# A table of head picks kept on chip, the compression's products set between head sums and transposes, and a memory sum that GpSimd prepares

## The reference, cut to what matters

```python
def rms_norm(x, g):
    return x * lax.rsqrt(jnp.mean(x * x, axis=-1, keepdims=True) + RMS_EPS) * g   # over 64 columns of a head
...
raw = (raw + cmp_pe[None, :, None]).reshape(B, 2, n_cmp, CMP_LEN * HEAD_DIM)      # 31 windows of 32 tokens
hid = jax.nn.gelu(jnp.einsum('bcnf,cfh->bcnh', raw, cmp_w1))                      # c: keys, values; 2048 -> 128
kv_c = jnp.einsum('bcnh,chd->bcnd', hid, cmp_w2)
...
y = ((y - m) * lax.rsqrt(var + GN_EPS)).reshape(B, T, D) * ln_g + ln_b            # group norm, heads of 64
...
memn = rmsnorm(mem, mem_norm_g)                                                   # 256 tokens, over 1024 columns
km, vm = split(memn @ w_kv)
```

## Time and profile before

| | before |
|---|---|
| median of three runs | 2717.42 us (2706.16 to 2719.36) |
| the profiled execution | 2718.71 us |
| its span, first to last instruction | 2716.9 us |
| PE / DVE / ACT / POOL busy | 95% / 44% / 34% / 37% |
| mean granted TensorE clock | 0.952 of full speed |
| moved by DMA | 196.96 MB, 72 GB/s |

### The profile page before, as it was taken

One profiled execution on the slowest core, in us unless ns is written; L12 is line 12 of the kernel. 1 busy time (PEld: TensorE's weight loads), 2 busy tenths in 40 slices (PEclk: granted clock), 3 DMA queues, 4 the chain that ended last, 5 costly groups with the idle time before them and its releaser, 6 DMA issues.

```text
span 2716.9 us, 32275 instructions
## 1 busy us (share of the span) xinstructions
PE 2582.6 (95%) x12202; PEld 1993.1 (73%) x12202; DVE 1193.4 (44%) x2017; ACT 936.8 (34%) x1580; POOL 1016.1 (37%) x611
## 2 busy tenths in 40 slices
PE   7999899999989988899899999999999999999997
PEld 6775477888836667788478788888766787888885
DVE  5112745213052665533253356336359733553362
ACT  3543643222245451222343333222422543322222
POOL 4331435444512221111065254534522452544344
PEclk9998699999989997888799999999999999999999
DMA  3222003333311110000232133323312321233231
GB/s 123 62 62 75 1 24 93 95 99 95 125 39 59 50 47 2 1 1 1 88 118 93 55 94 93 110 83 99 95 62 62 109 88 52 93 93 115 80 99 62
DMA packets 54415, 196.96 MB, mean 72 GB/s; under 512 B 6573, under 2 KB 6701, under 8 KB 53581
## 3 DMA queue, kind: packets, MB, share of 16 engines
q1 hardware_dynamic: 53312, 192.46, 22.9%
q10 hardware_dynamic: 974, 2.76, 0.3%
HBM read 193.10 MB, written 2.10 MB: 72 GB/s over the span
## 4 chain that ended last, share of the span: by engine, by line
PE 44%; DVE 5%; ACT 1%; DMA 0%; issue 0%; SPq 0%; POOLq 0%; POOL 0%; DVEq 0%; ACTq 0%
PE ps L386 10%; PE ps L387 10%; PE ps L388 10%; DVE ps L2815 3%; PE ps L374 3%; PE ps L375 3%; PE ps L376 3%; PE ps L2828 1%; PE ps L2658 1%; PE ps L2681 1%; DVE ps L2977 0%; DMA gwb<-in_lora_b 0%; PE ps L2427 0%; PE ps L2463 0%; PE ps L2434 0%
## 5 line engine op out<-in xcount | busy, mean ns | idle before, releaser
L507 POOL TENSOR_TENSOR w_lo<-raw,w_hi 128x1024 fp32r<-128x1024 f32 x342 | 819.7, 2406 | 1027.3 <-ACT w_hi L480 1027.1
L386 PE MATMUL ps<-ahead_hi,w_hi 128*128 128x512 f32 x1216 | 484.5, 398 | 1.1 <-DVE ahead_lo L609 1.1
L387 PE MATMUL ps<-ahead_lo,w_hi 128*128 128x512 f32 x1216 | 475.2, 391 | 0.0
L388 PE MATMUL ps<-ahead_hi,w_lo 128*128 128x512 f32 x1216 | 474.3, 390 | 0.0
L480 ACT ACTIVATE w_hi<-raw 128x1024 fp32r<-128x1024 f32 x342 | 353.0, 1049 | 171.8 <-PE ps L376 91.0
L386 PEld LDWEIGHTS ps<-ahead_hi,w_hi 128*128 128x128 f32 x1216 | 228.4, 188 | 54.5 <-issue 4.2
L387 PEld LDWEIGHTS ps<-ahead_lo,w_hi 128*128 128x128 f32 x1216 | 228.4, 188 | 51.5 <-issue 4.1
L388 PEld LDWEIGHTS ps<-ahead_hi,w_lo 128*128 128x128 f32 x1216 | 228.3, 188 | 51.0
L620 DVE TENSOR_TENSOR x_stream<-x_stream,ps 128x512 f32<-128x512 f32 x80 | 54.9, 687 | 466.7 <-PE ps L388 268.7
L374 PE MATMUL ps<-ffn_a_hi,w_hi 128*128 128x512 f32 x352 | 137.5, 390 | 2.9 <-DVE ffn_a_lo L2982 2.8
L2949 ACT ACTIVATE ffn_s<-ps 128x512 f32<-128x512 f32 x44 | 26.3, 598 | 326.8 <-DVE ps L2977 326.8
(11 more groups left out here) (419 smaller groups left out, 4772.5 us busy)
## 6 DMA issues: line engine op xcount, KB each, us to landing
raw<-in_wall SPq DMA_DIRECT2D x346, 512.0 KB, 3.6
x_stream<-in_x SPq DMA_DIRECT2D x8, 256.0 KB, 7.5
cw<-in_cmp_w SPq DMA_DIRECT2D x1, 2048.0 KB, 8.0
out_y<-x_stream SPq DMA_DIRECT2D x8, 256.0 KB, 2.2
lora_a<-in_lora_a ACTq DMA_DIRECT2D x1, 1152.0 KB
dist<-in_consts SPq DMA_DIRECT2D x1, 1088.0 KB, 10.0
mem<-in_mem SPq DMA_DIRECT2D x1, 1024.0 KB, 4.9
gwb<-in_lora_b SPq DMA_DIRECT2D x1, 1024.0 KB
```

The source lines that it names most:

```text
L386: pe.matmul(out, hi, src.hi[:, t, 0:width], start=first, stop=False)
L387: pe.matmul(out, hi, src.lo[:, t, 0:width], start=False, stop=False)
L388: return pe.matmul(out, lo, src.hi[:, t, 0:width], start=False, stop=last)
L507: e.tensor_tensor(self.w.lo[:, s, :], self.raw[:, s, :], as_float(self.w.hi[:, s, :]), ALU.subtract).then_inc(lo_r.sem, 1)
```

## The change

- The table of head picks is put a second time into the constants that stay on chip from the start (`own`, 38 columns; that load grows from 1025 to 1063 columns). The head sums and `variance` read it there, and PE's waits for the transfers ahead of them go; ahead of the gate's products a wait for `ld(32)` is added.
- In `prepare_mixers` the transfers are ordered anew: positions, `w1` in two halves of 64 partitions each with a semaphore of its own, then the 1320 constants, `w2`, distances.
- There, too, the ten head sums come first on PE. Behind each of the last four stand eight of the compression's first 32 products; the transposes follow, and behind each turn stand eight of the second 32. ACT squares all ten tiles, takes the root, and copies the turned values afterwards.
- In `GroupNorm` POOL adds the eight squared memory tiles in seven steps into the first, ahead of its two weight chunks, and PE makes one product with ones, behind the last variance.

```diff
-CONST_SIZES = [("ident", 128), ("blockones", 128), ("negtri", 128), ("m4", 512), ("cum", 129),
+CONST_SIZES = [("ident", 128), ("blockones", 128), ("negtri", 128), ("m4", 512), ("cum", 129), ("own", 4 * HEAD_TILES - 2),
...
+            sp.dma_start(pos[:, :], a["cmp_pe"]).then_inc(placed.sem, 16)
+            for half in range(2):
+                rows_ = slice(64 * half, 64 * half + 64)
+                sp.dma_start(w1[rows_, :, :], a["cmp_w1"][rows_, :, :]).then_inc(half_ld[half].sem, 16)
             sp.dma_start(far[:, c - N_KEEP:], a["consts"][:, c:N_CONST]).then_inc(picked.sem, 16)
-            sp.dma_start(pos[:, :], a["cmp_pe"]).then_inc(ld.sem, 16)
-            sp.dma_start(w1[:, :, :], a["cmp_w1"]).then_inc(ld.sem, 16)
             sp.dma_start(w2[:, :], a["cmp_w2"]).then_inc(ld.sem, 16)
...
-            for t in range(n):
-                if t < turns:
-                    turn(t)
-                if t == 0:
-                    pe.wait_ge(picked.sem, picked(16))
-
-                pe.wait_ge(sq_r.sem, sq_r(t + 1))
-                c = at("pick") + rows - 2 - 2 * t
-                pe.matmul(k.ps[0:rows, 0, :], far[:, c:c + rows], sq[:, t % 2, :], start=(t == 0), stop=(t == n - 1)
-                          ).then_inc(ss_r.sem, 1)
-
-            pe.wait_ge(raw_r.sem, raw_r(2))
-            for c in range(2):
+            def hidden(c, first, last):
+
+                if first == 0:
+                    pe.wait_ge(raw_r.sem, raw_r(2))
+                    pe.wait_ge(half_ld[c].sem, half_ld[c](16))
                 o = 64 * c
-                for j in range(32):
+                for j in range(first, last):
                     mm = pe.matmul(k.ps[0:N_CMP, 1 + c, 0:128], raw[o:o + 64, j, :], w1[o:o + 64, j, :],
                                    start=(j == 0), stop=(j == 31))
-                mm.then_inc(hs.sem, 1)
+                if last == 32:
+                    mm.then_inc(hs.sem, 1)
+
+            for t in range(n):
+                pe.wait_ge(sq_r.sem, sq_r(t + 1))
+                c = CST["own"] + rows - 2 - 2 * t
+                pe.matmul(k.ps[0:rows, 0, :], k.consts[:, c:c + rows], sq[:, t % 2, :], start=(t == 0), stop=(t == n - 1)
+                          ).then_inc(ss_r.sem, 1)
+                if t >= n - 4:
+                    hidden(0, 8 * (t - n + 4), 8 * (t - n + 4) + 8)
+            for i in range(turns):
+                turn(i)
+                hidden(1, 32 * i // turns, 32 * (i + 1) // turns)
...
                     pe.wait_ge(hc.sem, hc(1))
+                    pe.wait_ge(ld.sem, ld(16))
...
         @block.vector
         def _(v):
-            v.wait_ge(ld.sem, ld(48))
-
+            v.wait_ge(placed.sem, placed(16))
...
         def variance(m):
             pe.wait_ge(sq.sem, sq(m + 1))
-            if m == 0:
-                pe.wait_ge(ld.sem, ld(32))
-            c = HEAD_TILES * 2 - 2 - 2 * m
-            pe.matmul(k.ps[0:rows, 2, :], self.picks[:, c:c + rows], self.sqt[:, m % 2, :], start=(m == 0),
+            c = CST["own"] + HEAD_TILES * 2 - 2 - 2 * m
+            pe.matmul(k.ps[0:rows, 2, :], k.consts[:, c:c + rows], self.sqt[:, m % 2, :], start=(m == 0),
                       stop=(m == KD - 1)).then_inc(va.sem, 1)
...
-            if m == 4:
-                for n in range(KD):
-                    pe.wait_ge(squared.sem, squared(n + 1))
-                    mm = pe.matmul(k.ps[:, 4, 0:MEM], k.ones[:, :], self.sqm[:, n, :], start=(n == 0), stop=(n == KD - 1))
-                mm.then_inc(summed.sem, 1)
+        pe.wait_ge(self.added.sem, self.added(KD - 1))
+        pe.matmul(k.ps[:, 4, 0:MEM], k.ones[:, :], self.sqm[:, 0, :], start=True, stop=True).then_inc(summed.sem, 1)
+        pe.wait_ge(ld.sem, ld(32))
         self.gate(pe, 0)
...
     def gpsimd(self, g):
...
+        for n in range(1, KD):
+            g.wait_ge(squared.sem, squared(n + 1))
+            if n > 1:
+                g.wait_ge(self.added.sem, self.added(n - 1))
+            g.tensor_tensor(self.sqm[:, 0, :], self.sqm[:, 0, :], self.sqm[:, n, :], ALU.add).then_inc(self.added.sem, 1)
         for n in range(AHEAD):
```

More of the change, by code:

```diff
@@ L945, in prepare_mixers @@
         "cmp_rt", "cmp_inv", "cmp_done")
+    placed, *half_ld = k.sig("positions_loaded", "first_loaded", "second_loaded")
     at = lambda name: CST[name] - N_KEEP
@@ L1022, in _ @@
                 act.activation(sq[:, t % 2, :], pr[:, tiles[t][0], :], ACT.Square).then_inc(sq_r.sem, 1)
[L1023 to L1026, removed]
             act.wait_ge(ss_r.sem, ss_r(n))
@@ L1030, in _ @@
             act.activation(rt[0:rows, 0, :], k.ps[0:rows, 0, :], ACT.Sqrt, scale=scale, bias=bias).then_inc(rt_r.sem, 1)
+            for t in range(turns):
+                act.wait_ge(tr.sem, tr(t + 1))
+                act.activation(vt[:, :, t, :], k.ps[:, 4 + t % 4, :].rearrange("p (b d) -> p b d", b=NB), ACT.Copy
+                               ).then_inc(te.sem, 1)
             for c in range(2):
@@ L1070, in prepare_mixers @@
     for s, c in ((tr, turns), (te, turns), (picked, 16), (sq_r, n), (ss_r, n), (rt_r, 1), (inv_r, 1), (sp_r, n), (nr, n),
-                 (ld, 48), (raw_r, 2), (hs, 2), (ge, 2), (ht, 1), (hc, 1), (out_r, 2), (c1, 1), (c2, 1), (c3, 1),
-                 (c4, 1), (c5, 3)):
+                 (ld, 16), (raw_r, 2), (hs, 2), (ge, 2), (ht, 1), (hc, 1), (out_r, 2), (c1, 1), (c2, 1), (c3, 1),
+                 (c4, 1), (c5, 3), (placed, 16), (half_ld[0], 16), (half_ld[1], 16)):
         s.base += c
@@ L1351, in first_block @@
         low = k.low
-        k.retire("picks_loaded", "cmp_loaded", "cmp_raw", "cmp_hidden", "cmp_gelu", "cmp_turned", "cmp_turned_out", "cmp_out",
+        k.retire("picks_loaded", "positions_loaded", "first_loaded", "second_loaded", "cmp_loaded", "cmp_raw", "cmp_hidden", "cmp_gelu", "cmp_turned", "cmp_turned_out", "cmp_out",
                  "cmp_sq", "cmp_ss", "cmp_rt", "cmp_inv", "cmp_done", "z_ready", "softplus_steps", "softplus_log",
@@ L2385, in __init__ @@
         self.handed, self.fed = self.marks[12], self.memory[6]
+        self.added = k.marks("squares_joined")
+        k.advance(KD - 1, "squares_joined")
         self.slots = k.slots()
@@ L2506, in gpsimd @@
     def gpsimd(self, g):
-        k = self.k
+        k, squared = self.k, self.memory[0]
         hi_r, lo_r = self.splits
+        for n in range(1, KD):
[3 more added lines that the diff above has]
+            g.tensor_tensor(self.sqm[:, 0, :], self.sqm[:, 0, :], self.sqm[:, n, :], ALU.add).then_inc(self.added.sem, 1)
         for n in range(AHEAD):
@@ L3205, in constants @@
     u = np.arange(4 * HEAD_TILES - 2)[None] - (2 * HEAD_TILES - 2)
-    c["pick"] = (p // 64 == u)
+    c["pick"] = c["own"] = (p // 64 == u)
     c["spread"] = np.concatenate([(p == 2 * m + q // 64) for m in range(HEAD_TILES)], axis=1)
```

## The result

The changed kernel takes 2734.27 us (median of six, 2732.15 to 2735.86) against 2717.64 for the kernel before in the same comparison: a ratio of 1.0059, interval 1.0049 to 1.0070. It is 16.6 us slower, where 2700 was forecast, and outside the range. The profiled execution took 2735.86, with a span of 2734.2 against 2716.9. Runs over 1.5% above the fastest of the same kernel are left out of all ratios, such as one of 2920.29 among the ten of after_pad.

What follows compares the result with a forecast made beforehand. PE, busy 95% of the span, was taken to bound the kernel. Profiled execution 2718.71 less 5.9 (head sums and compression) less 11.9 (GroupNorm) gave 2700.9 us, hence a median of 2700, range 2689 to 2710.

Steps and rivals of the forecast that it cites:

- Head sums and compression, the work: In prepare_mixers: first sum starts at 224.25, PE's work takes 24.9 us and ends 5.9 us earlier.
- The landing of the weights: In prepare_mixers: first half of w1 landed at 228.4, second at 231; products begin behind seven sums, at 230.5.
- The half rate: Halves of w1 at half rate: first half lands at 230.9, costing 0.4 us; total 2701.3, chance 0.05.
- signs that I had named for being wrong: PE waiting ahead of the first products or for POOL at the memory's sum; clock low in windows where it was 1.00.
- The open part: Clock in prepare_mixers: taken to stay up; 1.7 us lost if it falls and returns, 3.4 at worst.
- the rival "slower": In prepare_mixers small products hold the clock down: PE ends 17 us later than before, total 2725.4; chance 0.03.
- The constants: The start's load of constants grows by 38 columns, 19 KB, costing 0.05 us.
- I expect nothing to be given back: Behind both changed stretches: what follows waits for work, not for times set outside, so the gains last.
- GroupNorm: In GroupNorm: last variance 12.3 us earlier, memory's sum costs 0.4, gain 11.9 us; Linear 24 us behind the first mean.
- The rival of the slow POOL: In GroupNorm: adds of 1.19 to 1.75 us, PE stands up to 3.7 us, gain 8.2, total 2704.6; chance 0.09.

Runs made afterwards that it cites:

- after_pad: The changed kernel with 96 unused columns behind the constants, ring of weights at 45696; 2723.69 us in the median of all ten runs.
- early_only: The changed kernel with the compression's first weights in two loads of 128 partitions, the first eight products' share first, no unused columns; 2712.39 us, ratio 0.9974.
- mix_early: after_align, mixed order kept, with the compression's first weights in two loads of 128 partitions, the first eight products' share first; 2696.36 us, ratio 0.9916.
- own_unused: The kernel before plus the 38 columns of the second pick table, loaded but read by nothing; 2728.87 us, ratio 1.0034.
- norm_alone: after_align with prepare_mixers of the kernel before, keeping the change in GroupNorm; 2702.69 us, ratio 0.9943.
- old_order: after_align with PE and ACT in the order of before in prepare_mixers, picks on chip, one load of the weights behind the positions; 2694.50 us, ratio 0.9917.
- after_align: The changed kernel with 48 unused columns, ring of weights at 45504; 2701.88 us.
- one_load: after_align with the compression's first weights in one load of 128 partitions and one semaphore in place of two halves; 2718.43 us, ratio 0.9992.
- sums_first: after_align with all ten head sums ahead of the first 32 products, the halves of the weights kept; 2697.35 us, ratio 0.9922.

## Why the prediction was wrong, point by point

The sum of what was measured, by medians: the place of the tiles costs 16.0 (early_only less mix_early) less what the kernel before already lost to it, 4.3, that is 11.7 us (own_unused alone: 10.1); GroupNorm wins 11.8; the first stretch loses 21.9, less the 6.3 that it wins where the clock stays up (norm_alone to mix_early), 15.6. Together 15.5, against 16.6 measured. That it comes so near is in part luck, for norm_alone stands in two of the terms, and 6 us moved between stretches there. The two profiles, before and after, need no such step: up to the first products on `cat` 18.7 us are lost, from there to GroupNorm 1.4 won, in GroupNorm 12.1 won, behind it 12.0 lost, 17.2 of the 17.3 in all.

- **Head sums and compression, the work.** Right in the main: 5.9 forecast, 6.3 by medians where no wait stands in front of the products, and some luck in it. From the first sum to the first spread 24.9 us were counted. old_order takes 24.94 without its first turn, which stands ahead of the sums there, and the mixed order of early_only 26.35: eight products between sums or turns take 1.86 us there, not 1.71. The first sum starts without a DMA.
- **The landing of the weights.** This step failed. I bounded PE's wait at 0.4 us, at half the rate, and it was 1.75. The half rate was right: 215 GB/s in the mean from 225 to 232, 437 in the window from 238, when the constants move over 128 partitions. The Trainium skill (SBUF — State Buffer, Door 1: The DMA port swizzle) states that 64 partitions in a row reach only half of the ports, and the trace agrees. But I counted 7.4 us from the positions' issue to the first half's landing, and it was 8.7. Most of the difference is the bytes. I let the first half have the whole rate. By 232, when it was about to land, 1.50 MB had moved, and its own are 1.05:

```profile
225.00:232.00 7.00, 5.44 (x13) 1.00 1.00 215
```

By the packets of the trace the 16 DMA engines were through with the first half's at different times, from 229.7 to 231.1, and the early ones went on with the second half's. So its bytes took 5.9 us (225.2 to 231.1) where the bound had 5.0; the fixed part was 2.7 in place of 2.4. The margin was zero to begin with: the products wanted at 230.4 what came at 232.1. PE's wait in front of the first products was one of the signs that I had named for being wrong.
- **The clock.** This step failed too, and by more. The open part was put at 3.4 us at worst in the forecast, where it cost some 20 (the 21.9 us between the changed kernel and early_only, less the wait), and only in the rival "slower" at the full price. That rival came true in its course (PE's last product late by 14.3 us in the profile, 17 foreseen, the low clock far into the next block), with a trigger that I had not given it: it should have hung on the wait in front of the products, which stood in my own working. I had asked what the wait costs, and not what the clock does behind it. Its chance of 0.03 was far too small. The Trainium skill (TensorE: Matmul & The Clock Gate, Part 4: PE-mode transpose) states that transposes do not count as busy for the clock. It explains nothing here: in mix_early the turns stand among products at 1.00, and no run here tests it.
- **The constants.** "0.05 us" for 38 columns was the cost of loading them. Their place in SBUF was not in the sum at all, nor in any rival, and it took 11.7 us: as much as GroupNorm won. "I expect nothing to be given back" failed on this.
- **GroupNorm.** Right in each step: 24.05 us against 24, 11.8 won against 11.9. The first variance starts 3.7 us behind the first mean, the clock rises 5.8 behind it (6.1 assumed, in the window 1342 to 1344 it is 0.88). Here a slip helped: the middle of 1323.9 and 1328.5 is 1326.2, not 1325.5. And what the clock does here is not fixed: in after_align, after_pad, old_order, norm_alone and one_load the means begin at the full clock and the stretch takes 21.9 us. POOL's adds take 0.73 each, 5.97 for seven with the waits between (5.3 assumed), and end 2.4 us ahead of the sum; the spare time was put at 3.3. The rival of the slow POOL is out.

## What to carry to other kernels

A table added to SBUF moves all that is placed behind it; before a change is judged by its instructions, place its tiles as they were (or pad), and compare the step between equal matmuls in a stretch that the change does not touch. A wait in front of TensorE has two prices, its length and what the clock does behind it, and the second was over ten times the first here; where work follows that has not been seen to lift the clock, a margin of nothing is a bet. Of two loads that are issued one behind the other, do not count on the first having the whole rate to itself until it has landed. Order loads by who reads them first and cut them by the free dimension, so that each piece keeps all 128 partitions.

## What the runs showed of the hardware that was not expected

- Equal matmuls (float32r, 128x128 against 512 columns, full clock) step by 227, 229, 232 or 233 ns as the moving tile lies 0, 64, 128 or 192 bytes, modulo 256, from the weights (128 on one tile only, whose distance no run changed).
- After a wait of 1.4 to 1.75 us the clock fell in some runs of a kernel and not in others: by their times, counting those above 2715, in five of nine of after_pad, four of ten of after_align, eight of ten of one_load, and in all six of the changed kernel. Behind the fall some 75 us of nearly gapless work on PE went by at 1.2 GHz. Without a wait ahead of the products the clock fell before the spreads in none of the 18 runs of sums_first, mix_early and early_only, by their times.
- The clock also falls with no wait: 1.9 to 4.4 us behind the first spread, in all profiles in which it was up until then.
- A load of 1024 KB to 64 partitions took 8.3 us to land, with 16 KB ahead of it and a second such load right behind it, one of 2048 KB to 128 partitions 7.9.
- The profiled runs of after_align (2685.75) and old_order (2682.36) are 10 to 11 us under the next run of their kernels. Between the first block and GroupNorm old_order's profile has a granted clock of 0.84 from 1000 to 1300 where sums_first has 0.82, in the recurrence, with the same code. With GroupNorm's start at the full clock this is the lowest of the three levels. What decides it is open, and it makes single runs of one kernel differ by 10 to 12 us.
